# Weights of V, Z and O in pairs of 256 columns, x tiles in places of their own, an earlier operand split and joined last quarters in a two-layer decoder step

## The reference

```python
def adaln(c, w, b):
    mod = jax.nn.silu(c) @ w + b
    shift, scale, gate = jnp.split(mod[:, None, :], 3, axis=-1)

for l in range(DEPTH):
    hp = rmsnorm(xp, g_pre[l]) * (1.0 + sc_p) + sh_p
    ...
    if l % 2 == 0:
        yp, kp, vp = attention_branch(hp, w_in_attn[j], w_out_attn[j], sinks[j])
    else:
        yp, Cp, npn, mp = mlstm_branch(hp, w_in_mlstm[j], b_if_mlstm[j], g_head_mlstm[j], w_out_mlstm[j], S0, n0, m0)
    xp = xp + gt_p * rmsnorm(yp, g_post[l])

def mlstm_branch(h, w_in, b_if, g_head, w_out, S0, n0, m0):
    proj = h @ w_in
    q, k, v, o, z, gates = jnp.split(proj, cuts, axis=-1)
    ...
    hn = hn * jax.nn.sigmoid(o) 
    out = hn * jax.nn.silu(z)
    y = out @ w_out
```

## Time and profile before

| | us |
|---|---|
| median of 3 runs | 2271.52 |
| lowest, highest | 2266.96, 2273.0 |
| the profiled execution | 2274.41 |
| its span | 2272.8 |
| TensorE busy | 2170.9 (96%) |
| VectorE busy | 940.9 (41%) |
| ScalarE busy | 677.5 (30%) |
| GpSimd busy | 74.9 (3%) |
| mean granted TensorE clock | 0.979 |

### The profile page before, as it was taken

The page is one execution under the profiler, slowest core; times in us unless marked ns, Lnnn a source line. Parts: engine busy times, 40 slices in busy tenths (PEclk is TensorE's granted clock), DMA queues, the critical chain, the costliest instruction groups (busy, mean ns, idle before and its releaser), DMA issues.

```text
span 2272.8 us, 37219 instructions
## 1 busy us (share of the span) xinstructions
PE 2170.9 (96%) x15828; PEld 1857.0 (82%) x15828; DVE 940.9 (41%) x1430; ACT 677.5 (30%) x1135; POOL 74.9 (3%) x125
## 2 busy tenths in 40 slices
PE   5899999999999999998899999999799999999998
PEld 2689999988999555567889999999799999985576
DVE  4434645456474422234443434443243434353223
ACT  4213534435252311126221222222222222231121
POOL 1000000000000100000000000000000000001000
PEclk8999999999999999998999999999899999999999
DMA  8972222232221788854425243534343344428622
GB/s 316 384 249 80 59 75 75 65 87 57 78 57 56 261 269 286 287 173 142 73 69 117 68 118 74 112 66 94 73 104 81 100 86 94 96 83 301 220 76 98
DMA packets 290435, 298.86 MB, mean 131 GB/s; under 512 B 8705, under 2 KB 213753, under 8 KB 288649
## 3 DMA queue, kind: packets, MB, share of 16 engines
q1 hardware_dynamic: 279504, 247.87, 39.6%
q0 software_dynamic: 10496, 48.45, 6.0%
q10 hardware_dynamic: 290, 0.32, 0.1%
HBM read 277.58 MB, written 23.11 MB: 132 GB/s over the span
## 4 chain that ended last, share of the span: by engine, by line
PE 84%; DMA 9%; DVE 3%; ACT 2%; issue 1%; ACTq 0%; DVEq 0%; SPq 0%
PE PJ L852 48%; PE PJ L1135 16%; DMA raw<-in_w_in_mlstm 6%; PE MX L1063 3%; DMA obuf<-in_w_ada 2%; PE PJ L876 2%; PE MX L992 1%; PE MX L1001 1%; PE MX L1101 1%; PE MX L1015 1%; ACT w_hi L1386 1%; PE MX L1269 1%; DVE w_lo L1842 1%; PE MX L955 1%; PE MX L1326 1%
## 5 line engine op out<-in xcount | busy, mean ns | idle before, releaser
L852 PE MATMUL PJ<-h_hi,w_hi 128*128 128x272 f32 x3200 | 684.8, 295 | 8.6 <-issue 6.9
L852 PE MATMUL PJ<-h_hi,w_lo 128*128 128x272 f32 x3200 | 667.5, 290 | 0.3 <-issue 0.3
L852 PE MATMUL PJ<-h_lo,w_hi 128*128 128x272 f32 x3200 | 665.6, 290 | 0.0
L852 PEld LDWEIGHTS PJ<-h_hi,w_hi 128*128 128x128 f32 x3200 | 507.0, 190 | 25.6 <-issue 20.8
L852 PEld LDWEIGHTS PJ<-h_lo,w_hi 128*128 128x128 f32 x3200 | 508.6, 191 | 7.0 <-issue 7.0
L852 PEld LDWEIGHTS PJ<-h_hi,w_lo 128*128 128x128 f32 x3200 | 505.6, 191 | 0.6 <-issue 0.6
L1842 DVE TENSOR_TENSOR w_lo<-raw,w_hi 128x2048 fp32r<-128x2048 f32 x106 | 242.9, 2292 | 389.0 <-ACT w_hi L1386 388.8
L1386 ACT ACTIVATE w_hi<-raw 128x2048 fp32r<-128x2048 f32 x106 | 202.3, 1909 | 86.9 <-DMA raw<-in_w_in_mlstm 64.2
L1135 PE MATMUL PJ<-w_hi,h_hi 128*128 128x512 f32 x512 | 216.1, 422 | 3.5 <-DVE w_lo L2117 2.3
L1135 PE MATMUL PJ<-w_hi,h_lo 128*128 128x512 f32 x512 | 202.9, 396 | 0.0
L1135 PE MATMUL PJ<-w_lo,h_hi 128*128 128x512 f32 x512 | 202.2, 395 | 0.0
(11 more groups left out here) (380 smaller groups left out, 2038.5 us busy)
## 6 DMA issues: line engine op xcount, KB each, us to landing
arena<-in_w_ada SPq DMA_DIRECT2D x64, 1024.0 KB, 5.2
raw<-in_w_in_mlstm SPq DMA_DIRECT2D x64, 1024.0 KB, 15.7
raw<-in_w_in_attn SPq DMA_DIRECT2D x40, 1024.0 KB, 5.8
obuf<-in_w_ada SPq DMA_DIRECT2D x32, 1024.0 KB, 11.4
raw<-in_w_out_attn SPq DMA_DIRECT2D x16, 1024.0 KB, 7.5
raw<-in_w_out_mlstm SPq DMA_DIRECT2D x16, 1024.0 KB, 5.2
arena<-in_state_C POOLq DMA_DIRECT2D x8, 1024.0 KB, 15.9
out<-arena POOLq DMA_DIRECT2D x8, 1024.0 KB, 5.9
```

The source lines that it names most:

```text
L852: last = mm(PJ[:, 2 * pair + f, 0:HT], w, h[:, k, HT * f:HT * f + HT], start=(k == 0 and n == 0), stop=(k == KT - 1 and n == 2))
```

## The change

- **x tiles.** Tile 3 has a place of its own, in the area sq (1536 columns) and scp (512); the sample tile goes to raw slot 0. The squares' waste goes to h_lo and their sums to st. GpSimd issues tile 3 once the first small product is done (vec_ps), the sample tile when tile 0 has been transposed. turn_x signals in halves (xt_done counts to 10), and the waits of SP follow.
- **Operand split.** The last entry before out0 and out1 signals h_free after k-step 3, and ScalarE's split_out of the first four blocks waits for that instead of the entry's end. At layer 1's end both engines make these four blocks ahead of memory step 6. The first sample product of out0 moves into unit 0; the sample products of units 1 to 3 stand at point 14 instead of 5. VectorE's split of unit 1's weights in out0 and out1 goes ahead of other work.
- **Last quarters.** Units 14 and 15 of both output products are run tile by tile in the order of `LAST_PARTS`, by a new function out_last. The rounding and the split of the gate's weights move behind x_scale(1, 0) and residual(0, 3).
- **Layer 1's weights.** L1K is "QKVVZZOO". For V, Z and O load_pair issues two DMAs of [128, 8 k, 256 columns] (rows of 1024 B), one half of the k-steps to each raw slot, when the entry before the pair has been split. round_hi and split_lo read such an entry with a stride from both halves (w_source) and wait for both landings. ScalarE's emptying of the second O waits until the first has been consumed.

The core of the diff:

```diff
-L1K = "QKVVZOZO"
+L1K = "QKVVZZOO"
...
-X_BUF, X_NTH = [0, 1, 2, 0, 1], [1, 1, 1, 2, 2]
+X_IN, X_NTH = [0, 1, 2, 3, 0], [1, 1, 1, 2, 2]
...
+        def w_source(ph, e):
+
+            if ph == "l1" and 2 <= e < len(L1K):
+                return raw_all.rearrange("p (k n) -> p k n", k=KT)[:, :, P * (e % 2):P * (e % 2) + P]
+            return raw[slot_of(ph, e)].rearrange("p (k n) -> p k n", k=KT)
...
                 if g < 2:
-                    sp.wait_ge(xt_done, 4 + g)
+                    sp.wait_ge(xt_done, 10 if g == 0 else 4)
...
+            def load_pair(it, e, col):
+
+                split = fixed(sp, unit_no("l1", it, e))
+                sp.wait_ge(xt_done, 10)
+                sp.wait_ge(lo_done, split)
+                for half in range(2):
+                    sp.dma_start(raw[half].rearrange("p (k n) -> p k n", k=KT // 2),
+                                 win1[:, KT // 2 * half:KT // 2 * (half + 1), ds(col, DV)]).then_inc(w_in[half], 16)
...
-                    load("l1", it, e, 0, win1[:, :, ds(h * width + (start[kind] + P * seen[kind]), P)])
+                    if kind in "QK":
+                        load("l1", it, e, 0, win1[:, :, ds(h * width + start[kind], P)])
+                    elif seen[kind] == 0:
+                        load_pair(it, e, h * width + start[kind])
...
             for t in range(5):
-                if t >= 3:
-                    pool.wait_ge(xt_done, t - 2)
...
+                elif t == 3:
+                    pool.wait_ge(vec_ps, 1)
...
                 else:
-                    pool.dma_start(x_rows[X_BUF[t]][0:TS, :], x_sample.rearrange("b t d -> (b t) d"))\
-                        .then_inc(x_in[X_BUF[t]], 16)
+                    pool.wait_ge(xt_done, 2)
+                    pool.dma_start(x_rows[4][0], x_sample.rearrange("b t d -> (b t) d")).then_inc(x_in[0], 16)
...
+                    elif k == 3 and frees:
+                        last.then_inc(h_free, 1)
...
+            LAST_PARTS = [(0, 14), (1, 14), (0, 15), (1, 15), (2, 14), (2, 15), (3, 14), (3, 15)]
+
+            def out_last(l, points):
+
+                ph, g = f"out{l}", 3
+                for part, (t, u) in enumerate(LAST_PARTS):
+                    q, s = u % 4, slot_of(ph, u)
+                    if part in (0, 2):
+                        pe.wait_ge(lo_done, UNIT0[ph] + u + 1)
+                    for i in range(4):
+                        k = 4 * q + i
+                        hi, lo = w_hi[s][:, 512 * i:512 * i + 512], w_lo[s][:, 512 * i:512 * i + 512]
+                        for n, (h, w) in enumerate(((h_hi, hi), (h_hi, lo), (h_lo, hi))):
+                            last = mm(PJ[:, bank_of(l, t), :], h[:, k, P * t:P * t + P], w,
+                                      start=False, stop=(k == KT - 1 and n == 2))
+                        if i == 3 and t == 3:
+                            last.then_inc(w_used, 1)
+                        elif i == 3 and u == 15:
+                            last.then_inc(y_made, 1)
...
-                for u in range(KT):
+                for u in range(KT - 2):
...
-                        points[5].append(lambda u=u: sample_product(l, u + 1))
+                        points[14 if u < 3 else 5].append(lambda u=u: sample_product(l, u + 1))
...
-            out_product(0, [lambda: sample_product(0, 0)], {})
+            out_product(0, [], {0: [(2, lambda: sample_product(0, 0))]})
...
                 act.wait_ge(w_in[s], landed_at(ph, it, e, j))
+                if ph == "l1" and 2 <= e < len(L1K):
+                    other = e + 1 - 2 * (e % 2)
+                    act.wait_ge(w_in[slot_of(ph, other)], landed_at(ph, it, other))
...
-                        act.wait_ge(w_used, ended(ph, it, e - 1))
+                        act.wait_ge(h_free, 1)
...
-            round_hi("gate", it0, 0)
             out_square(0, 3, 0)
...
+            x_square(1)
             x_scale(1, 0)
-            x_square(1)
+            round_hi("gate", it0, 0)
...
                 if kind == "O":
+                    if seen:
+                        act.wait_ge(*freed_at("l1", it, e - 1))
...
+                            if it[0] is None and it[1] == MH - 1 and p == 6:
+                                act.wait_ge(h_free, 2)
+                                act.wait_ge(head_done, 3)
+                                split_out(range(4))
...
                 split_out(3, range(8, 12))
+            ahead(1, 1)
```

More of the change, by code:

```diff
@@ L240, in trunk @@
         obuf = sb("obuf", [P, KT, T])
-        raw = [sb(f"raw{i}", [P, D]) for i in range(2)]
+        raw_all = sb("raw", [P, 2 * D])
+        raw = [raw_all[:, D * i:D * i + D] for i in range(2)]
         w_hi = [sb(f"w_hi{i}", [P, D], F32R) for i in range(2)]
@@ L526, in load @@
                 s = slot_of(ph, e, j)
-                split = fixed(sp, unit_no(ph, it, e, j - 1))
-                sp.wait_ge(xt_done, 5)
+                split = fixed(sp, unit_no(ph, it, e, j - 1 + (ph == "l1" and e == 0 and it[0] is not None)))
+                sp.wait_ge(xt_done, 10)
                 sp.wait_ge(lo_done, split)
@@ L839, in entry, with block @@
                 pe.wait_ge(lo_done, unit_no(ph, it, e) + 1)
-                block(s, pair, points, h_base)
-            def block(s, pair, points, h_base):
+                block(s, pair, points, h_base, frees)
+            def block(s, pair, points, h_base, frees):
                 if h_base == 2 * KT:
@@ L1049, in layer0 @@
                             points[k] = lambda p=p: attend(m, p)
-                    entry(ph, it, e, points)
+                    entry(ph, it, e, points, frees=(ph == "l0z" and e == len(L0Z) - 1))
             layer0("l0p", it0, None)
@@ L1142, in out_unit @@
                             f()
+            LAST_PARTS = [(0, 14), (1, 14), (0, 15), (1, 15), (2, 14), (2, 15), (3, 14), (3, 15)]
[15 more added lines that the diff above has]
+                            last.then_inc(y_made, 1)
+                        for f in points.get((part, i), ()):
+                            f()
             def out_product(l, first, points0):
@@ L1339, in layer1 @@
                             points[k] = gate_turn
-                    entry("l1", it, e, points)
+                    entry("l1", it, e, points, frees=(it[1] == MH - 1 and e == len(L1K) - 1))
             layer1((None, 0), None)
@@ L1385, in round_hi @@
                     return
-                fn(w_hi[s][:, :], raw[s][:, :], ACT.Copy).then_inc(hi_done, 1)
+                fn(w_hi[s][:, :].rearrange("p (k n) -> p k n", k=KT), w_source(ph, e), ACT.Copy).then_inc(hi_done, 1)
             def mod_copy(n):
@@ L1841, in split_lo @@
                 else:
-                    tt(w_lo[s][:, :], raw[s][:, :], w_hi[s][:, :].bitcast(F32), ALU.subtract)\
-                        .then_inc(lo_done, 1)
+                    tt(w_lo[s][:, :].rearrange("p (k n) -> p k n", k=KT), w_source(ph, e),
+                       w_hi[s][:, :].bitcast(F32).rearrange("p (k n) -> p k n", k=KT), ALU.subtract).then_inc(lo_done, 1)
             def mod_empty(ph, e, n):
@@ L2217, in _ @@
             out_product(0)
-            split_lo("gate", it0, 0)
             dve.wait_ge(mod_taken, 13)
@@ L2233, in _ @@
             residual(0, 3)
+            split_lo("gate", it0, 0)
             x_scale(3, 2)
```

114 lines of the change are left out of this document (62 added, 52 removed).

## The result

| | before | after |
|---|---|---|
| median, us | 2272.26 (4 runs) | 2355.68 (4 runs) |
| lowest to highest | 2266.96 to 2274.9 | 2354.07 to 2357.19 |
| ratio | | 1.037, 95% interval 1.035 to 1.0391 |
| profiled span | 2272.8 | 2355.6 |
| mean granted TensorE clock | 0.979 | 0.958 |

The change costs 83 us. The forecast was a gain (2248), with 2212 to 2310 as range: both were wrong.

What follows compares the result with a forecast made beforehand. The prediction took the kernel as a stream of matmuls with TensorE busy 96%. Layer 1's pairs -7, x tiles -5.5, operand split -7 and last quarters -4.5 gave -24 us on 2274.4, lowered to the median: 2248 us, range 2212 to 2310.

Steps and rivals of the forecast that it cites:

- The bound: Whole kernel: a stream of matmuls, TensorE busy 96%, about 100 us to win; heads 0 and 4 lose 47 us.
- The forecast of 11 to 14 us for Z's pairs: Layer 1: Z and O pairs land in 11 to 14 us, fitting windows of 14.6 and some 17 us.
- The window of V: Layer 1, undisturbed head: 16.0 us from the V pair's issue to when its weights must have landed.
- Its price: Layer 1's V pair: lands like the present second V load, 14.8 to 21.0 us, late by 12.6 us in all.
- rival 2: Layer 1's V pair takes 20 to 21 us in seven heads, 4.5 us stops each: 2295 us, chance 0.24.
- The window of O: Layer 1's O pair has some 17 us until the previous head's VectorE and ScalarE work queues up behind it.
- the slower rival: Another wording for rival 2, the slower side: the window closes at V, 2295 us, chance 0.24.
- Heads 0 and 4: Layer 1's two slow heads: pairs stop the queue being outrun, gaining 6 us in head 0, 12 in head 4.
- The factor of 1.5: Layer 1: each us of idle TensorE time was charged as 1.5 us lost.
- The order: Layer 1: ScalarE's tanh of the second O waits for the first to be consumed; costs nothing unless VectorE lags an entry.
- The other edits: Edits outside layer 1's loads: x tiles -5.5, operand split -7, last quarters -4.5 us, together -17.

Runs made afterwards that it cites:

- e7: Changed kernel, each DMA of a pair reading only 128 columns a row (same packets, half the bytes; second halves of V, Z, O left out): 2326.2 us.
- e6: Changed kernel with seven of the eight state_C loads cut to an eighth of their bytes: 2347.2 us, ratio 1.0328.
- e4: Changed kernel with single loads in place of layer 1's pairs, the order QKVVZZOO kept: 2229.4 us, ratio 0.9822.
- e3: Changed kernel with the half of the V pair that goes into Q's raw slot issued an entry earlier: 2290.6 us, ratio 1.0086.
- e8: Kernel of e4 with its single loads issued at the pairs' points, when the entry before each two has been split: 2398.4 us, ratio 1.0557.
- e1: Changed kernel with layer 1's single loads and order QKVVZOZO as before, all other edits kept: 2252.9 us, ratio 0.9913.
- e9: Kernel of e1 with its loads reading columns in the order VVZZOO while the work stays ZOZO (two entries get wrong weights): 2232.4 us, ratio 0.9833.
- e5: Kernel of e4 with the nine small sinks DMAs moved behind the last bias row of ada0: 2224.4 us, ratio 0.9789.
- e12: Kernel before with only the nine sinks DMAs moved behind the last bias row of ada0: 2270.7 us, ratio 0.9996.
- e10: Kernel of e4 with the last quarters of both output products unit by unit as before: 2235.0 us, ratio 0.9836.
- e11: Kernel of e4 with the operand split, sample products and out1's unit-1 weights back in their old places: 2239.9 us, ratio 0.9867.

## Why the prediction was wrong

**The bound** was read rightly: a stream of matmuls in which the weight DMAs of layer 1 are the largest loss, heads 0 and 4 the worst. That packets more than bytes are paid held (e7). The forecast of 11 to 14 us for Z's pairs held only in heads 1 and 5; the others took 14.8 to 24.6 us, and the three rows behind the forecast (11.9 to 13.7 us, head 1) were themselves the fast ones: the present first Z load of head 2 took 19.1 us, that of head 3 16.5, that of head 5 22.0. That rounding in pieces of 128 columns costs nothing held: 1909 ns for L1442 and 2291 for L1909, as before.

**The window of V** was worked out as 16.0 us, and it is: issue at 1205.85, TensorE ready at 1226.25, less 4.2 for rounding and splitting, so 16.2. **Its price was the step that failed.** I put in the landing of the present second V load (16.4 in head 1), taking equal packet counts for equal times. The pair took 20.6, 19.7, 22.9, 25.5, 17.1, 18.7 and 22.3 us in heads 1 to 7, that is 3 to 5 us more in six of the seven. The forecast had 12.6 us of lateness in all; the stops before V0 are 40.7. Two things are in it: the second DMA is issued 0.56 us after the first, and twice the bytes beside the state's traffic (e7 2.5 us, e6 4.1 us in head 1). The upper bound I had for this, 20 to 21 us, was my rival 2, at 2295.

**The window of O** was the second failing step. "Some 17 us until the previous head's work queues up" had no row behind it. In head 1 ScalarE is ready 11.4 us after the issue (1273.8 - 1262.4); the pair took 13.9. TensorE then stops not for the weights but at the recurrence (L1322), 1.5 to 6.5 us in every head, 27.3 us in all on the page; before, it stopped there only in heads 0 and 4, 4.2 and 5.1 us. That is also why even the slower rival was too mild.

**Heads 0 and 4** were to gain 6 and 12 us. They lost: head 0's V-to-V stretch went from 137.0 (1080.2 to 1217.2) to 151.4, those of heads 3 and 4 together from 253.1 (1430.17 + 18.05 to 1683.27 + 18.05, by the chain's markers) to 278.6. In heads 0 and 4 every pair takes 21 to 26 us to land, in windows of 15 to 17, and head 0 alone has stops of 7.7 us before V0, 12.3 before Z0 and 5.7 at the recurrence. With one load always ahead such a head runs at the pace of its loads (e4: 22 to 26 us with two under way, a load every 10 to 18); with a pair it pays landing plus entries in turn. I had seen that the queue is outrun in these heads and concluded that fewer packets would mend it; what mattered, as e3 and e8 bear out, was that the queue must not run dry while TensorE works, and with pairs it does (DMA share 0.29 in head 0, 0.38 before). Why loads are slower in these two heads than in the others, no run shows.

**The factor of 1.5** from idle to lost time held roughly: 53 us more idle, 83 lost, 1.57. These sums mix the pairs' loss with the other edits' gain; of *after* against e1 it is 72 idle and 102 lost, 1.40, against e4 87 and 130, 1.50. It is no constant: in e6 16 us less idle brought 8 us.

**The order** was costed at nothing; it gains 23 us (e4 against e1, e9). I looked at it only for ScalarE's wait on the second O, and not for which loads meet in the queues. The Trainium skill ("DMA: Bandwidth & Descriptors", Latency and other measured facts) suspects aliasing of memory channels for a pitch of 4 MiB between partitions, and has full speed again with 4 KiB more. Here the pitch between partitions is 32832 B, so what it measured isn't this case. e1 and e4 (33.5 against 23.6 us) show that where two loads stand to each other matters here, and no run shows the channels themselves. By the Trainium skill ("DMA: Bandwidth & Descriptors", How a descriptor splits into AXI transactions), a pair would have cost an estimated 5/3 of a load, 20 us. The trace doesn't bear that out as a rule for time: in head 1 the Z pair took 12.8 us with rows of 1024 B and 12.1 with rows of 512 B (e7).

**The other edits**: -17 forecast, -19.4 measured. Inside, the operand split was worth 10 us (forecast 7) and the last quarters 3 to 5.5 (forecast 4.5). The **x tiles** were worth nothing, where -5.5 was forecast: the last wait for h_lo moved from 133.46 to 134.07, and the entries behind it from 147.1 to 148.5. The hole in the DMA share was taken for SP's wait alone; the sinks' DMAs, issued from 21.3 to 26.5 us, kept it open (e5, e12). The rest of the 19.4, some 4 to 6 us, is not assigned; e10 and e11 were measured on e4's order of loads, and each difference is that of two medians.

**The sum**, by runs:

| step | us | difference |
|---|---|---|
| before | 2272.3 | |
| split, last quarters, x tiles (e1) | 2252.9 | -19.4 |
| order ZZOO (e4) | 2229.4 | -23.4 |
| loads issued at the pairs' points (e8) | 2398.4 | +169 |
| rows of 1024 B instead of 512 (after) | 2355.7 | -43 |

The version to keep is e5: the change without its pairs but with their order, and the sinks' DMAs out of the way, 2224.4 us, 2.1% below the kernel before (e4, without the last of these, is as good within the noise).

## What to carry to other kernels

A buffer that is refilled only when all of it is free turns a stream of loads into load and wait in turn: before widening a transfer at the cost of a slot, compare the window from its issue to its use with the slowest landing of that stretch, not with the median of the narrow one, and for every engine that waits on it, not only for the one that consumes it. When DMAs are slow with idle queues, look at which addresses are read together, and not only at how wide the rows are: here that was worth 23 us. And a hole in the DMA share can have two causes, so that taking one away pays little or nothing.
